# Two mixture-of-experts layers on one core: the router, the lists of rows and the summing rewritten

## What is computed

```python
def hier_moe(h, w_group, b_group, w_expert, b_expert, w1, w3, w2):
    t, d = h.shape
    pg = jax.nn.softmax((h @ w_group).astype(jnp.float32) + b_group.astype(jnp.float32), axis=-1)
    g_prob, g_idx = lax.top_k(pg, 1)
    le = ((h @ w_expert).astype(jnp.float32) + b_expert.astype(jnp.float32)).reshape(t, N_GROUPS, EXPERTS_PER_GROUP)
    le = jnp.take_along_axis(le, g_idx[:, :, None], axis=1)[:, 0]
    e_prob, e_idx = lax.top_k(jax.nn.softmax(le, axis=-1), TOP_K)
    weights = g_prob * e_prob / jnp.sum(e_prob, axis=-1, keepdims=True)
    expert_id = g_idx * EXPERTS_PER_GROUP + e_idx
    ...
        return (jax.nn.silu(xb @ w1[e]) * (xb @ w3[e])) @ w2[e]
    ...
    return jnp.zeros_like(h).at[stok].add(y)
```

## Time and profile before

| | us |
|---|---|
| median of 3 executions | 4538.05 |
| lowest, highest | 4532.4, 4543.82 |
| the profiled execution's own time | 4529.35 |
| its span, first to last instruction | 4527.6 |
| PE busy in it | 3847.3 (85%) |
| DVE, ACT, POOL busy | 1552.4, 1342.3, 227.3 |
| mean granted TensorE clock | 0.926 |

### The profile page before, as it was taken

How to read it: one execution, slowest core, us unless ns; L and a number is a source line. 1 busy time by engine, 2 the same in 40 slices (tenths; PEclk the granted TensorE clock), 3 DMA queues, 4 the chain that set the end, 5 groups by cost and what they waited for, 6 DMA issues and landing times. The chain is left out here.

```text
span 4527.6 us, 76374 instructions
## 1 busy us (share of the span) xinstructions
PE 3847.3 (85%) x32368; PEld 2191.1 (48%) x32368; DVE 1552.4 (34%) x3792; ACT 1342.3 (30%) x2928; POOL 227.3 (5%) x221
## 2 busy tenths in 40 slices
PE   5999577777787899999988959999959988699996
PEld 2555366666665445665566543333335455333332
DVE  2000366666665013442346221111132183211112
ACT  2000234444433022332446222222225262122221
POOL 0000000000000000010100010000012000100000
PEclk7999799899998899999999969999979999799998
DMA  5221444344442220000210059999933101799996
GB/s 202 74 92 48 129 114 119 101 118 118 117 114 68 83 104 1 19 19 28 64 45 1 1 193 341 380 380 379 358 128 94 44 1 41 279 380 380 379 377 248
DMA packets 450869, 697.52 MB, mean 154 GB/s; under 512 B 168762, under 2 KB 191448, under 8 KB 450008
## 3 DMA queue, kind: packets, MB, share of 16 engines
q1 hardware_dynamic: 428600, 613.83, 39.2%
q0 software_dynamic: 14752, 53.53, 3.6%
q10 hardware_dynamic: 7168, 25.17, 1.4%
HBM read 625.57 MB, written 64.54 MB: 152 GB/s over the span
## 5 line engine op out<-in xcount | busy, mean ns | idle before, releaser
L196 PE MATMUL ps<-arena 128*128 128x384 f32 (+9 forms) x5598 | 1619.9, 454 | 192.0 <-issue 38.7
L196 PEld LDWEIGHTS ps<-arena 128*128 128x128 f32 (+4 forms) x5598 | 935.2, 195 | 844.5 <-issue 456.3
L2631 PE MATMUL ps<-arena 128*32 128x512 f32 x9216 | 1038.1, 604 | 44.5 <-DMA arena<-in_w 39.9
L2631 PEld LDWEIGHTS ps<-arena 128*32 128x32 f32 x9216 | 307.4, 111 | 677.2 <-issue 660.3
L572 PE MATMUL ps<-arena 64*64 64x64 f32 (+1 forms) x10624 | 462.4, 241 | 177.1 <-DVE arena L1133 61.4
L572 PEld LDWEIGHTS ps<-arena 64*64 64x64 f32 x10624 | 413.6, 146 | 256.1 <-issue 100.7
L202 PE MATMUL ps<-arena 128*128 128x128 f32 x1200 | 197.0, 301 | 98.7 <-DVE arena L3033 46.1
L2765 DVE COPY arena<-ps 128x384 f32<-128x384 f32 x64 | 35.7, 557 | 675.9 <-PE ps L2690 675.9
L2741 ACT ACTIVATE arena<-ps 96x512 f32<-96x512 f32 x64 | 38.0, 593 | 651.8 <-PE ps L2631 651.8
L202 PEld LDWEIGHTS ps<-arena 128*128 128x128 f32 x1200 | 148.9, 157 | 142.9 <-DVE arena L3033 49.5
L545 DVE SCALAR_TENSOR_TENSOR arena<-arena 128x768 f32<-128x768 f32 x48 | 45.1, 1013 | 350.5 <-PE ps L196 350.5
(11 more groups left out here) (277 smaller groups left out, 3646.2 us busy)
## 6 DMA issues: line engine op xcount, KB each, us to landing
arena<-in_w SPq DMA_DIRECT2D x192, 2048.0 KB, 22.6
arena<-in_w_mod SPq DMA_DIRECT2D x24, 2048.0 KB, 8.9
arena<-in_mod_w SPq DMA_DIRECT2D x12, 2048.0 KB, 15.8
yb<-arena ACTq DMA_DIRECT2D x64, 384.0 KB, 6.3
arena<-in_rwkv_w_in SPq DMA_DIRECT2D x8, 2048.0 KB, 11.0
rkvg<-arena POOLq DMA_DIRECT2D x32, 384.0 KB, 2.6
arena<-rkvg SPq DMA_DIRECT2D x32, 384.0 KB, 4.0
arena<-di SPq DMA_DIRECT2D x192, 64.0 KB, 2.4
```

Source lines behind the costliest of these rows:

```text
L196: ins = pe.matmul(out, l, r, start=(i == 0), stop=(i == len(pairs) - 1))
L2631: return pe.matmul(bank[32 * at:32 * at + 32, :], left[:, k, 32 * g:32 * g + 32], right[:, k, :], start=first, stop=last)
```

## The change

In both layers:

- The router's 36 columns become the stationary side and H the moving side: 16 products in layer 0 (512 and 256 tokens wide) and 8 in layer 1, in place of 48 and 32. The result has tokens along the free side, is copied to `LT` (ACT, and DVE for the context part) and transposed back by PE, 6 or 4 small transposes into one bank. The bias is added by one instruction.
- The turning of H now uses four banks and four buffers `HTOK`; PE turns tiles 0 and 1 ahead of the counting and the others behind it.
- DVE first only chooses (`dve_choice`) and sets the masks. The exponentials' use and the weights move behind the list (`dve_weights`), together with the numbers of the spare blocks (`dve_more`). Counting takes 7 wide products in place of 27 narrow ones in layer 0, and 5 in place of 14 in layer 1. The two mask arrays are one, and the overflow test is one comparison and one reduction.
- The table in DRAM, its blanking, the 12 or 8 scatters and the read back go. DVE makes for each tile and choice two 0/1 matrices, `A` (token by block) and `S` (token by place in the block, with the token's number for 1), and PE sums S transposed times A over the 12 or 8, which is the list.
- Four more small tables are loaded by SP, and PE waits for nine loads, not five.
- In the sum, all 12 or 8 gathers are issued without waits, into the loop's slots 2 to 4. ACT does the first scaling (`Copy` with a scale), for all tiles ahead of the squares of the next layer's sums.
- The last store is four DMAs, one for each tile of 128 tokens (rows of 512 bytes), each when its tile is added.

The diff, cut to its core:

```diff
     put("tri", np.triu(np.ones((128, 128)), 1))
-    put("eidx", np.tile(np.arange(32)[None, :], (128, 1)))
+    put("eidx", np.tile(96.0 * np.arange(32)[None, :], (128, 1)))
+    put("over", np.tile(96.0 * (31 - np.arange(32))[None, :], (128, 1)))
+    put("edge", np.tile(96.0 * np.arange(52)[None, :] - 0.5, (128, 1)))
+    put("place", np.tile(np.arange(96)[None, :] - 96.0, (128, 1)))
+    put("more", np.tile(96.0 * np.arange(1, 9)[None, :] + 0.5, (128, 1)))
...
+        self.GA = [self.slots[2 + i // 4][:, 1024 * (i % 4):1024 * (i % 4) + 1024] for i in range(2 * tiles)]
+
+        early = K.top
+        self.LT = K.take(T)
+        self.A1, self.A, self.S = K.take(2 * tiles, self.NB + 1), K.take(2 * tiles, self.NB), K.take(2 * tiles, ROWS)
...
-        self.HTOK = K.take(2, D)
+        self.HTOK = [K.take(D), K.take(D), *self.YS]
...
+    def stored(self, e):
+
+        for j in range(4):
+            e.wait_ge(self.hstored[j], 16 * ((self.tiles + 3 - j) // 4))
...
-        sp.wait_ge(self.cleared, 1)
-        sp.dma_start(self.blank_rows(), self.tab[0:self.NB, :]).then_inc(self.blank, 16)
...
+    def pe_turn(self, pe, first, last):
+
+        for i in range(2 * first, 2 * last):
+            tt, c = divmod(i, 2)
+            if i >= 4:
+                pe.wait_ge(self.hevac, i - 3)
+            turn4(pe, self.hbank(i), [self.norm.H[:, k, tt * 128:(tt + 1) * 128] for k in range(4 * c, 4 * c + 4)], self.K.C("ident")
+                  ).then_inc(self.hturned, 1)
...
-            for tt in range(self.tiles):
-                ins = pe.matmul(ps[:, 2 + tt, 0:36], H[:, k, tt * 128:(tt + 1) * 128], self.wr[:, k, :], start=(k == 0), stop=(k == KT - 1),
-                                skip_group_check=True)
+            for j, (a, n) in enumerate(self.segments()):
+                ins = pe.matmul(ps[0:36, 2 + j, 0:n], self.wr[:, k, :], H[:, k, a:a + n], start=(k == 0), stop=(k == KT - 1), skip_group_check=True)
                 if k == KT - 1:
                     ins.then_inc(self.logits, 1)
...
-        pe.wait_ge(self.logged, self.tiles)
-        pe.wait_ge(self.masked, 1)
-        for tt in range(self.tiles):
-            mm(pe, ps[:, 2, 32 * tt:32 * tt + 32], [(K.C("ones"), self.M[:, u, :]) for u in range(tt)] + [(K.C("tri"), self.M[:, tt, :])])
-        mm(pe, ps[:, 2, 256:288], [(K.C("ones"), self.M[:, u, :]) for u in range(self.tiles)]).then_inc(self.counted, 1)
-        pe.wait_ge(self.table, 16)
-        pe.transpose(ps[0:ROWS, 3, 0:self.NB], self.tab[0:self.NB, :], K.C("ident")[0:self.NB, 0:self.NB]).then_inc(self.listed, 1)
+        for tt in range(tiles):
+            if tt in (0, 4):
+                pe.wait_ge(self.levac[tt // 4], 1)
+            ins = pe.transpose(ps[:, 4, 36 * tt:36 * tt + 36], self.LT[0:36, 128 * tt:128 * tt + 128], K.C("ident")[0:36, 0:36])
+        ins.then_inc(self.lturned, 1)
+        self.pe_turn(pe, 0, 2)
+
+        pe.wait_ge(self.masked, 2)
+        n = 32 * (tiles + 1)
+        flat = self.M.rearrange("p t e -> p (t e)")
+        pe.matmul(ps[:, 2, 0:n], K.C("tri"), flat, start=True, stop=False, skip_group_check=True)
+        for u in range(1, tiles + 1):
+            ins = pe.matmul(ps[:, 2, 32 * u:n], K.C("ones"), flat[:, 0:n - 32 * u], start=False, stop=(u == tiles), skip_group_check=True)
+        ins.then_inc(self.counted, 1)
+        self.pe_turn(pe, 2, tiles)
+        for i in range(2 * tiles):
+            pe.wait_ge(self.chosen, i + 1)
+            ins = pe.matmul(ps[0:ROWS, 3, 0:self.NB], self.S[:, i, :], self.A[:, i, :], start=(i == 0), stop=(i == 2 * tiles - 1))
+        ins.then_inc(self.listed, 1)
         pe.wait_ge(self.index, 1)
...
+        act.wait_ge(self.experts, 3)
+        for tt in range(self.tiles):
+            A = self.GA[2 * tt]
+            act.wait_ge(self.got[2 * tt], 16)
+            act.activation(A, A, ACT.Copy, scale=self.WTS[:, 0, tt:tt + 1]).then_inc(self.weighed, 1)
         if after:
...
+        self.dve_choice(dve)
         self.dve_places(dve)
         dve.wait_ge(self.listed, 1)
         dve.tensor_copy(self.IDX[0:ROWS, 0:self.NB], ps[0:ROWS, 3, 0:self.NB]).then_inc(self.index, 1)
+        self.dve_more(dve)
+        self.dve_weights(dve)
         self.blocks.dve(dve)
...
-            dve.wait_ge(self.got[q0], 16 * (tt // 2 + 1))
-            dve.tensor_scalar(A, A, self.WTS[:, 0, tt:tt + 1], None, ALU.mult).then_inc(self.mixed, 1)
-            dve.wait_ge(self.got[q1], 16 * (tt // 2 + 1))
-            dve.wait_ge(self.mixed, 2 * tt + 1)
+            A, B = self.GA[2 * tt:2 * tt + 2]
+            dve.wait_ge(self.got[2 * tt + 1], 16)
+            dve.wait_ge(self.weighed, tt + 1)
             dve.scalar_tensor_tensor(A, B, self.WTS[:, 1, tt:tt + 1], A, ALU.mult, ALU.add).then_inc(self.mixed, 1)
...
+        did(dve.tensor_tensor(self.A1, D_.unsqueeze(2).broadcast_to([128, 2 * tiles, nb + 1]), bcast(K.C("edge")[:, 0:nb + 1], 2 * tiles), ALU.is_ge))
+        dve.wait_ge(self.gate, did.n)
+        did(dve.tensor_reduce(blk.unsqueeze(2), self.A1, AX.X, ALU.add))
+        did(dve.tensor_tensor(self.A, self.A1[:, :, 0:nb], self.A1[:, :, 1:nb + 1], ALU.subtract))
+        dve.wait_ge(self.gate, did.n)
+        did(dve.scalar_tensor_tensor(blk, blk, -float(ROWS), D_, ALU.mult, ALU.add))
+        dve.wait_ge(self.gate, did.n)
+        for i in range(2 * tiles):
+            dve.tensor_scalar(self.S[:, i, :], K.C("place"), blk[:, i:i + 1], K.C("tokid")[:, i % tiles:i % tiles + 1], ALU.is_equal, ALU.mult
+                              ).then_inc(self.chosen, 1)
...
-        pool.wait_ge(self.placed, 1)
-        pool.wait_ge(self.blank, 16)
-        pool.wait_ge(self.tables, 80)
-        for j in range(2):
-            for tt in range(tiles):
-                pool.indirect_dma_start(out=tabd.unsqueeze(1)[0:self.NB * ROWS, :],
-                                        out_offset=bass.IndirectOffsetOnAxis(ap=self.DIX[:, j, tt:tt + 1], axis=0),
-                                        in_=K.C("tokid")[:, tt:tt + 1], in_offset=None).then_inc(self.scattered, 16)
-        pool.wait_ge(self.scattered, 32 * tiles)
-        pool.dma_start(self.tab[0:self.NB, :], self.blank_rows()).then_inc(self.table, 16)
-        for i in range(2):
-            pool.wait_ge(self.hstored[i], 8 * tiles)
+        self.stored(pool)
         pool.wait_ge(self.index, 1)
...
+        for i in range(2 * tiles):
+            tt, j = divmod(i, 2)
+            pool.indirect_dma_start(out=self.GA[i], out_offset=None, in_=K.scr["yb"][0:self.NB * ROWS, :],
+                                    in_offset=bass.IndirectOffsetOnAxis(ap=self.DIX[:, j, tt:tt + 1], axis=0)).then_inc(self.got[i], 16)
...
-            moe.over(sp)
-            sp.dma_start(K.out.rearrange("(k p) t -> p k t", p=128), K.X[:, :, 0:TX]).then_inc(K.s["stored"], 16)
-            sp.wait_ge(K.s["stored"], 16)
+            for tt in range(4):
+                at = slice(128 * tt, 128 * tt + 128)
+                sp.wait_ge(moe.added, 8 * (tt + 1))
+                sp.dma_start(K.out.rearrange("(k p) t -> p k t", p=128)[:, :, at], K.X[:, :, at]).then_inc(K.s["stored"], 16)
+            sp.wait_ge(K.s["stored"], 64)
```

248 lines of the change are left out of this document (120 added, 128 removed).

## The result

| | before | after |
|---|---|---|
| median, us | 4538.62 (4 executions) | 4467.59 (4 executions) |
| lowest, highest | 4532.4, 4543.82 | 4460.23, 4473.1 |
| the profiled execution's own time | 4529.35 | 4466.63 |
| its span | 4527.6 | 4464.8 |
| mean granted TensorE clock | 0.926 | 0.938 |

The changed kernel takes 0.9843 of the time before (95% interval 0.9824 to 0.9862), 71 us less by the medians. The forecast was 4474 with a range of 4458 to 4498. The spans of the two profiled executions differ by 62.8 us, and the forecast's own sum was 64.0. What the sum's terms did is a separate question, since two sums can agree with their terms apart.

The account below looks back on a forecast made before the run. It took the chain from scoring to the first gather to delay block 0, ahead of loops full on DMA and PE. Terms 37.7 + 23.9 - 3 + 2.5 + 2.9 = 64.0 us off 4538.05 gave 4474, range 4458 to 4498.

Parts of the forecast that it names:

- The path: Ahead of each layer's loop: each us that block 0 starts earlier is a us off the span; 37.7 and 23.9 us.
- Its condition: Ahead of the loop's ninth load, which waits for block 0, the DMA engines still have an idle stretch; 9 us left.
- Scoring: Router products on PE at the routing's start: 13.4 us in layer 0, before 20.67, the clock rising from half to full.
- The rival in which it stays low: PE's clock stays at half while scoring, which takes 21.1 and 14.1 us; kernel at 4486, chance 0.14.
- Choosing, counting, list: Routing after scoring, layer 0: masks at 2644.1, counting done at 2647.6, list at 2660, behind PE's other turnings of H.
- Stores and gather: Routing's end, both layers: the last htok store, not the list, comes last, landing in 6.4 us; first gather 7.8 us.
- Sum, layer 0: After layer 0's loop: 1.8 us off by shorter periods, tile 0's square on ACT 4.8 later; net 3 us lost.
- Sum, layer 1, and tail: Layer 1's sum 2.5 us off, with a scaling moved to ACT; output store in four pieces 2.9 us off.
- the rival of a gain given back: The ninth load, waiting for slots 6 and 7, caps the gain; both loops lose half of it: 4505, chance 0.08.
- that of slower slots: Loads in both loops slow down as slots lie about 100 columns further on; at 6.0 us each 4551, chance 0.03.
- The queues: Rival: stores at 8.4 and gathers at 10.8 us in both layers, 2 more in the sum: 4486 to 4490, chance 0.12.

## Why the prediction was right

**The path.** The argument that block 0's start moves the end one for one held for what was changed: routings 59.1 us shorter, against 61.6 forecast. Its condition held too, in layer 1 only just. 9 us of idle DMA were forecast to be left ahead of the ninth load, worked out for layer 0 and used for both. In layer 0, 6.7 are left, and in layer 1 some 1.4. The kernel with slots 4 to 7 held shows what happens when they are used up.

**Scoring.** 13.4 and 9.7 us were forecast, 13.27 and 9.36 measured, with the clock rising inside it. The rival in which it stays low is out. But by the kernel with the old router, the 11.9 us of both layers are worth only some 3.6. The forecast hadn't priced that edit alone. It had said that the store comes last, from which this follows.

**Choosing, counting, list.** Each was a little faster than forecast. The masks came 7.0 us after scoring, not 8.4. The counting ended 10.9 after scoring, where 11.9 was forecast. The last store went out 16.6 after scoring, not 20.3, mostly since PE's 32 turnings took 4.71 us at a rising clock, not 7.4. The list was ready 21.4 after scoring, not 24.3. The list's own gain on the forecast didn't count, as its slack of 5 us shows. What moved the last store did: it bought the 3.7 us that the next step needed.

**Stores and gather.** This step carried the routing, and it was right in kind: the store comes last in both layers. In size its two halves missed, and one miss was made good by the step before. The first gather followed the last store by 10.3 and 9.7 us, where 6.6 was taken from the median of stores before. The gather took 9.51 and 7.49, where 7.8 was taken. The stores before ran mostly on half idle engines, these beside six fills. In layer 0 the store was issued 3.7 us sooner than worked out and landed 3.7 later, which cancels. The gather's 1.7 us are what is left, and that routing missed by 1.5.

**Sum, layer 0.** This term was mis-sized: 3 us lost were forecast, and some 0.6 are gained (3.3 in the profile shown). Its mechanism, PE's wait for ACT's square in tile 2, is there. Against the end of the loop, the squares come 2.9 us later than before in the median of eight profiles, where 4.8 was worked out. The step that gave the 4.8 took six gathers to land in 7.4 us at half the rate up to the eleventh, ending at 3322, 29.7 us after the loop's last store of `yb`. In the changed kernel ACT's last scaling, which waits for the eleventh gather, begins 27.4 us after it. The other half of the miss is the periods: "some 8.2; over three tiles, 1.8 us off" is 2.5 to 3.9 off (26.2 and 26.3 before, 22.4 to 23.7 after) and 4.5 in the one profile in which the clock rose furthest.

**Sum, layer 1, and tail.** 2.5 forecast, 3.3 measured in the pair, 2.5 between the medians of all profiles: DVE's period fell from 5.42 to 4.56 us. And 2.9 against 4.2 for the store: a 512 KB piece landed in 3.2 us, not the 4.4 of the one row of that size. That row was of a load from DRAM. The fit in the Trainium skill (DMA: Bandwidth & Descriptors, Anatomy of one DMA) gave an estimated 3.2 for a quarter, which the trace agrees with, although the page gives it for DMAs issued by GpSimd and these are issued by SP. The rule of the Trainium skill on batching to 1 MiB (the same page, Bandwidth) spoke against four pieces. Here they ended the kernel 4.2 us sooner, since only the last piece is waited for.

**The rivals.** The loop didn't lengthen beyond what repeats show, so neither the rival of a gain given back nor that of slower slots has anything for it in this trace. The idle time left in layer 1 shows that the first of them was near. The queues did cost more than taken, by 3.7 and 1.7 us in layer 0, but faster steps ahead hid most of that. That is luck in the sum rather than insight.

## What to carry to other kernels

When a chain of waits is shortened, what is left at its end is usually a transfer, and the transfer then runs beside loads that used to wait. Price it under load, not by its times in the idle engines of before; a scatter's last landing went from 1.5 to 7.4 us that way. Removing one wait of a chain is worth only up to the next thing in its way, another engine's own order of work or a transfer: moving the weights alone gave 5.7 us of 21.5, and the faster router some 3.6 of 11.9. When two profiles are compared, look first whether they already differ ahead of the edit. In layer 1 up to 2.2 us did. And a start that is made earlier by holding loads back is paid back in a loop that runs at the full DMA rate.

## What the hardware showed that I had not expected

- Scattering and reading back small elements suffers more from loads beside it than bulk does: the last landing went from 1.5 to 7.4 us (9.4 in layer 1), and the read back from 2.0 to 4.9. A gather of 96 rows of 4 KB went from 4.6 to 9.5, and 512 KB stores from a median of 6.4 to 8.0.
- In a stage of short bursts of PE, the granted clock differed from one execution to the next. With 3.77 us of pause it was 0.50 in the first two sums of the kernel before. With 2.59 us it was 0.87 and 0.83 in one profile of the changed kernel, and the sum of 16 small products took 2.6 us there. In others it took up to 3.79. The three periods of that stage came to 21.8 to 23.7 us with the same code.
- Products with only 36 stationary columns and 512 moving ones were granted the full clock 5.6 us after their start in layer 0 of the first profile, as products with 128 were at some 5. In layer 1 of the kernel with its first gather ahead of slots 6 and 7 it was 2.9 us. With the same code ahead of it, this moved the last store of `htok` by 2.2 us from one profile to another.
